# The first tiles behind three inner norms computed from x times its column scale, and another order in the mixer and the drain

## What is computed

```python
def rms_norm_2(x, g):  # x * rsqrt(mean(x*x) + eps) * g
def modulate(h, shift, scale): return h * (1.0 + scale) + shift
mod = silu(c) @ ada_w + ada_b        # shift, scale, gate of three parts, D numbers each
h = modulate(rms_norm_2(x, norm_g[0]), shift0, scale0)
x = x + 0.5 * gate0 * ((silu(h @ Wg) * (h @ Wu)) @ ffn1_w_out)
h = modulate(rms_norm_2(x, norm_g[1]), shift1, scale1)
x = x + gate1 * token_mixer(h)
h = modulate(rms_norm_2(x, norm_g[2]), shift2, scale2)
x = x + 0.5 * gate2 * ffn2(h)
return rms_norm_2(x, final_g)
```

## Time and profile before

| | us |
|---|---|
| median of 3 runs (lowest, highest) | 1940.26 (1938.29, 1940.6) |
| the profiled execution, its own time | 1941.78 |
| its span from first to last instruction | 1939.9 |
| busy: TensorE / VectorE / ScalarE / GpSimd | 1882.2 / 932.9 / 800.3 / 125.6 |
| mean granted clock of TensorE | 0.987 |

### The profile page before, as it was taken

How to read it: one execution, slowest core, us unless ns; L and a number is a source line. 1 busy time by engine, 2 the same in 40 slices (tenths; PEclk the granted TensorE clock), 3 DMA queues, 4 the chain that set the end, 5 groups by cost and what they waited for, 6 DMA issues and landing times.

```text
span 1939.9 us, 22192 instructions
## 1 busy us (share of the span) xinstructions
PE 1882.2 (97%) x8907; PEld 1457.4 (75%) x8907; DVE 932.9 (48%) x1665; ACT 800.3 (41%) x1301; POOL 125.6 (6%) x148
## 2 busy tenths in 40 slices
PE   7999999999999899999998999999999999999997
PEld 4666666666788788888886777687788878888886
DVE  4567666665542433333225566854434443333322
ACT  5466656656542332222223655434432332222221
POOL 0111111110001000000000011000000100000000
PEclk8999999999999999999998999999999999999999
DMA  5334333432233132222223222221023322222221
GB/s 207 148 142 152 141 141 142 152 141 89 76 132 108 65 109 98 98 98 90 101 72 125 93 71 92 75 84 44 32 94 114 121 76 97 98 98 95 100 90 63
DMA packets 56525, 201.94 MB, mean 104 GB/s; under 512 B 6478, under 2 KB 6934, under 8 KB 55784
## 3 DMA queue, kind: packets, MB, share of 16 engines
q1 hardware_dynamic: 44616, 158.32, 23.3%
q0 software_dynamic: 11808, 42.21, 5.9%
HBM read 195.23 MB, written 5.28 MB: 103 GB/s over the span
## 4 chain that ended last, share of the span: by engine, by line
PE 77%; DVE 11%; ACT 9%; issue 2%; DMA 1%; DVEq 0%; SPq 0%; ACTq 0%
PE ps L1016 22%; PE ps L1019 22%; PE ps L1017 22%; ACT wH L1665 2%; DVE wL L1300 2%; PE ps L1105 2%; DVE a L1388 1%; PE ps L1069 1%; DVE a L1544 1%; ACT a L1750 1%; PE ps L1093 1%; PE ps L1081 1%; PE ps L1141 1%; PE ps L1040 1%; DVE g1a L1300 1%
## 5 line engine op out<-in xcount | busy, mean ns | idle before, releaser
L1016 PE MATMUL ps<-hH,wH 128*128 128x512 f32 (+1 forms) x1640 | 667.5, 407 | 19.7 <-DVE hL L1340 12.3
L1019 PE MATMUL ps<-hH,wL 128*128 128x512 f32 (+1 forms) x1640 | 645.6, 394 | 0.7 <-DVE wL L1300 0.7
L1017 PE MATMUL ps<-hL,wH 128*128 128x512 f32 (+1 forms) x1640 | 645.1, 393 | 0.0
L1300 DVE TENSOR_TENSOR wL<-wr,wH 128x1024 fp32r<-128x1024 f32 (+2 forms) x285 | 345.3, 1212 | 579.1 <-ACT wH L1665 579.0
L1665 ACT ACTIVATE wH<-wr 128x1024 fp32r<-128x1024 f32 (+2 forms) x285 | 295.0, 1036 | 265.5 <-PE ps L1019 245.6
L1016 PEld LDWEIGHTS ps<-hH,wH 128*128 128x128 f32 (+1 forms) x1640 | 311.0, 190 | 118.2 <-issue 47.8
L1019 PEld LDWEIGHTS ps<-hH,wL 128*128 128x128 f32 (+1 forms) x1640 | 310.5, 189 | 70.1 <-DVE wL L1300 2.1
L1017 PEld LDWEIGHTS ps<-hL,wH 128*128 128x128 f32 (+1 forms) x1640 | 311.4, 190 | 63.3 <-issue 3.4
L1016 PE MATMUL ps<-gffn,wH 128*128 128x512 f32 x352 | 136.9, 389 | 0.0
L1017 PE MATMUL ps<-gffn,wH 128*128 128x512 f32 x352 | 136.9, 389 | 0.0
L1019 PE MATMUL ps<-gffn,wL 128*128 128x512 f32 x352 | 136.9, 389 | 0.0
(11 more groups left out here) (283 smaller groups left out, 1971.1 us busy)
## 6 DMA issues: line engine op xcount, KB each, us to landing
wr<-wst SPq DMA_DIRECT2D x268, 512.0 KB, 3.4
a<-wfd POOLq DMA_DIRECT2D x54, 512.0 KB, 4.8
xT<-wfd POOLq DMA_DIRECT2D x18, 512.0 KB, 6.6
wr<-wst SPq DMA_DIRECT2D x16, 384.0 KB, 2.9
xT<-xin SPq DMA_DIRECT2D x8, 256.0 KB, 4.8
xT<-xin SPq DMA_DIRECT2D x2, 1024.0 KB, 6.2
xsave<-xT SPq DMA_DIRECT2D x1, 2048.0 KB, 8.9
c<-wfd POOLq DMA_DIRECT2D x8, 256.0 KB, 3.0
```

The lines of the kernel that those rows point to most:

```text
L1016: e.matmul(o, hi, xh[k], start=k == 0, stop=False)
L1017: e.matmul(o, hi, xl[k], start=False, stop=False)
L1019: i = e.matmul(o, lo, xh[k], start=False, stop=k == t.nk - 1)
L1300: e.tensor_tensor(dst, x, hi.bitcast(F32), ALU.subtract).then_inc(s[name], 1)
```

## The change

For the three inner norms the first tiles no longer wait for rs. While the residual tiles run, `raw` makes X[c]*scale (rounded part on ScalarE, rest on VectorE), and `raw_start` issues the first two tiles (three in the feed-forwards) on these; the sum of squares of c=7 stands behind their second k step. The row scale rs is multiplied in at the bank's output, and the shift's part comes as a bias: `shift_row` (eight chained operations 128x128 on VectorE, from the raw weights) and `shift_sum` (fp32 matmuls with ones) give shift*W for each such tile. The usual norm is made beside these tiles, in two halves (`norm_c`) with a weight split between. At n=2 the raw parts lie in hH and hL themselves, so `norm_c` on ScalarE waits for the products of each k (`rm`).

In the same change: `sq_lo` and `rstd` of the last two heads' outputs 4 steps later; pool tiles 0 and 1 of the mixer raw, `feed_pool` behind them, and the save of x behind `baturn`; `l2_sum` 3 ticks later, `l2` 2, `l2_end` 3, `prep_x` 3, `prep_k` and `prep_q` 2, `sol_send` 2, `solve` spread over 90 in place of 75 ticks, `sol_back` and `inverse` 18 later; three banks (6, 7, 0) for `rec_o`; the sum of the squares of n=1 in a tile of its own; one semaphore for several in two places.

```diff
+    def raw(self, n, c):
+        self.add("raw", n=n, c=c, rh=self.sig("rh"), rl=self.sig("rl"))
+    def shift_row(self, n, i, slot):
+        self.add("shift_row", n=n, i=i, slot=slot, wb=self.sig("wb"))
+    def shift_sum(self, n, count):
+        self.add("shift_sum", n=n, count=count, rows=self.count["wb"], modt=self.sig("modt"), wb=self.sig("wb"))
+        self.shb = self.count["wb"]
+    def raw_start(self, n, t0, t1, t2=None):
+        tiles = [t for t in (t0, t1, t2) if t is not None]
+        self.slot(t0, 0)
+        self.slot(t1, 0)
+        for k in range(8):
+            if k == 2:
+                self.last_square()
+                self.raw(n, 7)
+            self.add("mm", t=t0, k=k)
+            self.add("mm", t=t1, k=k, raw=self.sig("rm") if k < 7 else None)
+        if t2 is not None:
+            self.slot(t2, 0)
+            for k in range(8):
+                self.add("mm", t=t2, k=k)
+        for t in tiles:
+            t.done = t.slots[-1] + 1
+        rs = self.sig("rs")
+        self.add("norm_rs", n=n, stat=8 + 2 * n, rs=rs)
+        self.add("norm_c", n=n, c0=0, c1=5, rs=rs, raw=t1)
+        self.add("split", j=t0.slots[0] + NSPL)
+        self.add("norm_c", n=n, c0=5, c1=8, rs=rs, raw=t1)
+        self.add("split", j=t1.slots[0] + NSPL)
+        for name in ("nv", "nh", "nl"):
+            self.count[name] = self.count.get(name, 0) + 8
+        for i, t in enumerate(tiles):
+            if i == 2:
+                self.add("split", j=t2.slots[0] + NSPL)
+            self.add("out_" + t.kind, t=t, done=t.done, raw=i, rs=rs, last=tiles[-1].done, shb=self.shb, **t.more)
...
-                put(0, sq_lo, o3, "o")
-                put(SCHED["o"], rstd, None, o3)
+                put(0 if o3 < HEADS - 2 else 4, sq_lo, o3, "o")
+                put(SCHED["o"] if o3 < HEADS - 2 else 9, rstd, None, o3)
...
+        first = len(self.slots) + 16
+        more = {4: [lambda: add("mod_rest"), lambda: self.raw(1, 0), lambda: self.raw(1, 1)],
+                5: [lambda c=c: self.raw(1, c) for c in (2, 3, 4)], 6: [lambda: self.raw(1, 5)], 7: [lambda: self.raw(1, 6)]}
+        at = {(6, 9): lambda: self.shift_row(1, 0, first), (7, 1): lambda: self.shift_row(1, 1, first + 1),
+              (7, 8): lambda: self.shift_row(1, 2, first + 2), (7, 13): lambda: self.shift_sum(1, 3)}
         for c in range(8):
             r = sig("xr")
-            self.whole(Tile("res0", src("l0_w_out", 128 * c, 16), self.pb01.take()[1], "g", ("xr", r), c=c, xr=r),
-                       then=(lambda: square(c - 1)) if c > 0 else None)
+            t = Tile("res0", src("l0_w_out", 128 * c, 16), self.pb01.take()[1], "g", ("xr", r), c=c, xr=r)
+            for k in self.steps_of(t):
+                if k == 5 and c > 0:
+                    square(c - 1)
+                    for fn in more.get(c, []):
+                        fn()
+                if (c, k) in at:
+                    at[c, k]()
...
+        self.raw_start(n, gate(0, "r"), up(0, "r"), gate(1, "r"))
+        self.whole(up(1))
+        for j in range(2, 22):
+            self.whole(gate(j))
+            self.whole(up(j))
...
+        first = len(self.slots) + 24
         for c in range(8):
             r = sig("xr")
-            self.whole(Tile("res", src(w_out, 128 * c, 22), pb.take()[1], "a", ("xr", r), c=c, xr=r, sub=sub, f=f, back=None),
-                       then=(lambda: square(c - 1)) if c > 0 else None)
-        square(7)
+            t = Tile("res", src(w_out, 128 * c, 22), pb.take()[1], "a", ("xr", r), c=c, xr=r, sub=sub, f=f, back=None)
+            for k in self.steps_of(t):
+                if k == 5 and c > 0:
+                    square(c - 1)
+                    if n == 1:
+                        self.raw(2, c - 1)
+                if n == 1 and c == 7 and k in (2, 9):
+                    self.shift_row(2, k // 9, first + k // 9)
+                if n == 1 and c == 7 and k == 16:
+                    self.shift_sum(2, 2)
+        self.last_square = lambda: square(7)
...
-        self.two(pool(0), pool(1))
+        self.raw_start(n, pool(0, "r"), pool(1, "r"))
+        add("feed_pool")
         t = Tile("ba", src("mix_w_in_2", 4608, cols=16), wk.take()[1], "h", ("bd", 1), n=n)
         self.whole(t)
         for k in self.steps_of(pool(2)):
             if k == 5:
                 pool_mid(0)
         add("baturn", bank=wk.take()[1])
+        self.move("saved")
...
-                at(end + 10 + j, l2_sum, h, l2s)
+                at(end + 13 + j, l2_sum, h, l2s)
                 if which == "k":
-                    at(end + 16 + 2 * j, prep_x, h)
-                    at(end + 34 + 2 * j, prep_k, h)
+                    at(end + 19 + 2 * j, prep_x, h)
+                    at(end + 36 + 2 * j, prep_k, h)
                 else:
-                    at(end + 36 + 2 * j, prep_q, h)
-            at(end + 15, l2, which, l2s)
-            at(end + 23, l2_end, which, l2s)
+                    at(end + 38 + 2 * j, prep_q, h)
+            at(end + 17, l2, which, l2s)
+            at(end + 26, l2_end, which, l2s)
...
-        at(121, lambda: add("sol_send", pa2=8))
+        at(123, lambda: add("sol_send", pa2=8))
         for k in range(1, 31):
-            at(133 + (5 * k) // 2, lambda k=k: add("solve", k=k))
-        at(209, lambda: add("sol_back"))
+            at(135 + 3 * k, lambda k=k: add("solve", k=k))
+        at(227, lambda: add("sol_back"))
         for g in range(2):
             for j, step in enumerate(("t", "p5", "y5", "p6", "y6")):
-                at(233 + 16 * g + 3 * j, inverse, g, step)
+                at(251 + 16 * g + 3 * j, inverse, g, step)
...
-        rk, ro, rm = Ring([3, 4, 5]), Ring([6, 7]), Ring([1, 2])
+        rk, ro, rm = Ring([3, 4, 5]), Ring([6, 7, 0]), Ring([1, 2])
...
+        def behind(c):
+            square(c)
+            self.raw(3, c)
+            if 3 <= c < 6:
+                self.shift_row(3, c - 3, first + c - 3)
+            elif c == 6:
+                self.shift_sum(3, 3)
         for c in range(8):
             r = sig("xr")
             self.whole(Tile("res", src("mix_w_out_2", 128 * c), pb6.take()[1], "m", ("xr", r), c=c, xr=r, sub=1, f=None,
-                            back=c // 4), then=(lambda: square(c - 1)) if c > 0 else None)
-        square(7)
+                            back=c // 4), then=(lambda: behind(c - 1)) if c > 0 else None)
+        self.last_square = lambda: square(7)
...
+        def raw_views(n):
+            if n == 2:
+                return rhs["h"]
+            a = ff[0]["aH"][0:16] if n == 1 else ff[1]["aH"][16:22] + ff[1]["aL"][0:10]
+            return a[0:8], a[8:16]
+        def shift_rows(n, i):
+            return {1: row1, 2: ff[0]["row"], 3: tq[1]}[n][:, 128 * i:128 * i + 128]
...
+                if t.rhs == "r":
+                    w.wait_ge(s["rl"], 8 * (t.more["n"] - 1) + k + 1)
...
+                elif what == "shift_sum":
+                    b = take(6)
+                    bank_free[6] = ("wb", d["wb"])
+                    w.wait_ge(s["wb"], d["rows"])
+                    for j in range(d["count"]):
+                        i = e.matmul(b[:, 2 * j:2 * j + 2], shift_rows(d["n"], j), C("one", 0, 2), start=True, stop=True)
+                    i.then_inc(s["modt"], 1)
...
+                elif what == "raw":
+                    n, c = d["n"], d["c"]
+                    xh, xl = raw_views(n)
+                    w.wait_ge(s["rh"], d["rh"])
+                    e.scalar_tensor_tensor(xl[c], X[c], scale_col(n, c), xh[c].bitcast(F32),
+                                           ALU.mult, ALU.subtract).then_inc(s["rl"], 1)
+                elif what == "shift_row":
+                    n, j = d["n"], d["slot"]
+                    v, acc = split_views(j)[0], shift_rows(n, d["i"])
+                    w.wait_ge(s_raw[j % NRAW], 16 * (j // NRAW + 1))
+                    own(e.tensor_scalar(acc, v[:, 0:128], shift_col(n, 0), None, ALU.mult, ALU.bypass))
+                    for k in range(1, 8):
+                        own_done()
+                        i = e.scalar_tensor_tensor(acc, v[:, 128 * k:128 * k + 128], shift_col(n, k), acc, ALU.mult, ALU.add)
+                        if k < 7:
+                            own(i)
+                    i.then_inc(s["wb"], 1)
+                elif what == "shift_sum":
+                    w.wait_ge(s["modt"], d["modt"])
+                    e.tensor_copy(shb[:, 0:2 * d["count"]], ps[6][:, 0:2 * d["count"]]).then_inc(s["wb"], 1)
+                elif what == "norm_c":
+                    n, c0, c1 = d["n"], d["c0"], d["c1"]
+                    rs, tmp = norm_views(n)
+                    w.wait_ge(s["rs"], d["rs"])
+                    for c in range(c0, c1 + 1):
+                        if c < c1:
+                            if c >= 2:
+                                w.wait_ge(s["nl"], 8 * n + c - 1)
```

(53 more changed lines are left out.)

117 lines of the change are left out of this document (68 added, 49 removed).

## The result

The median after is 1914.70 us (1914.08 to 1916.92, 4 runs) beside 1940.01 us (4 runs) of the kernel before: a ratio of 0.9873, 95% interval 0.9856 to 0.9890, so 25.3 us less. The forecast was 1910.6, 29.7 less. The profiled execution after took 1915.1 us (span 1913.3), 26.7 less than the one before. The sum came out near, in part by luck: one of its six terms, the mixer's events with 8.8 us, was worth nothing, and four of the others paid more than I had put down.

A forecast was written before the change was run, and what follows sets the result against it. TensorE was taken as the bound, so only its idle or slow time could be won. The terms 3.2 + 3.3 + 6.7 + 8.8 + 4.3 + 3.4 = 29.7 us gave median 1910.6 us, range 1905 to 1918 (8 in 10: 1903 to 1922).

The forecast's parts named there:

- the mixer's events: Mixer: l2_sum 3 ticks later removes most of four waits for squares and slow products: 8.8 us, ends 4.5 and 10.
- What bounds it: Whole kernel: TensorE, busy 1882 of 1939.9 us, is the bound; only its idle or slow time can be won.
- n=1: Norm behind out0: raw start gains 8.1 us, less shift sum, a wait and slow clock: net 3.2, ends 1.9 and 7.3.
- n=2: Norm before the mixer: two raw tiles, waits for pool weights and baturn's copy: net 3.3 us, ends 1.1 and 6.1.
- n=3: Norm behind the mixer: raw start gains 8.1 us, less 0.8 and 0.6: net 6.7, ends 4 and 7.3.
- The drain and the bank: Drain: later sq_lo and rstd, 4.3 us (2.5 to 4.6); recurrence: third bank removes three waits, 3.4 us (at least 2).
- My own line on what would prove me wrong: Wrong if a split waits within 12 us of a norm, clock falls without a pause, or l2 waits move elsewhere.
- A: At n=1 and n=2 the clock stays up and pool weights come in time: 35 us gain, 1905; chance 0.17.
- B: VectorE takes the norm's place: boundaries lose 1.5 us and a clock fall each, l2's fourth wait stays: 1925; chance 0.10.
- C: Only mixer and drain count; raw starts wait for their own rows, boundaries give 0: 16.5 us gain, 1924; chance 0.07.
- D: Whole kernel slower: without pauses the chip lowers TensorE's clock; 250 slow products give 1961 us; chance 0.02.

The follow-up runs named there:

- the other ring: Changed kernel plus taps ahead of the weight split, solve and inverse earlier, n=1 column sum at k=15, n=3 PSUM ring from bank 2: 1903.30 us, ratio 0.9812.
- prep early: Changed kernel with prep_k and prep_q two ticks earlier, at end + 34 and end + 36: 1915.46 us, ratio to before 0.988.
- sum at k=15: Changed kernel with the shift's column sum at n=1 at k=15 instead of k=13 of the last tile: 1911.75 us, ratio to before 0.9863.

## Why the prediction came out as it did

*What bounds it*: right for the whole. TensorE was and is the bound, and the gain is what it no longer idles or runs slowly. Not right for the sessions of the mixer, where ScalarE and VectorE together set the pace (42.95 against 41.5 us).

*n=1*: 3.2 forecast, 3.8 measured. The wait before the shift sum, its reason and the clock's fall behind it were as worked out; the wait was 1.7 us instead of 2.1, since VectorE met no add of GpSimd there, and eight products were slow instead of ten. In the one execution without the fall the stage gave 5.0.

*n=2*: 3.3 forecast, 5.7 in this trace and 4.2 where the clock fell behind the wait for the weights. The three waits of the 16-column tile were two, 1.7 instead of 2.3. The pool weights were there at T+27.6, where I had 28.2. The copy for baturn ended at T+29.4, where I had 29.6 (my terms add to 29.5), but TensorE came to it only at T+30.0 and waited for nothing. I had put one stretch of low clock behind the wait for the weights; in after it lay ahead, from 1034.28 on, and the wait swallowed it.

*n=3*: 6.7 forecast, 6.0 measured. No wait at the shift sum. The 0.6 that I took off for VectorE's lateness did turn up as 0.98, at a place that I hadn't looked at: the residual that frees the second tile's bank. The experiment with the other ring shows it (1.27 us by starts).

*The drain and the bank*: 4.3 and 3.4 forecast, 4.5 and 4.2 measured, the same alone by stage. The bank's term was the sum in the table of waits, which leaves out some 0.3 us of each pause.

*The mixer's events*: 8.8 forecast, below even my lower end of 4.5; 1.2 against the profile before, and -0.2 against three kernels with the old ticks. This is the step that failed: "Moving l2_sum by 3 ticks of three products is 2.05 us of TensorE's time. Three of the four waits are 1.0 to 1.3 us and go whole." I took four waits for four separate latenesses, each to be covered by the same 2.05 us. They were one: the chain of ScalarE and VectorE fell behind TensorE by about 1.4 us a session. A later l2_sum is covered once; what it doesn't wait in session 1 is missing in session 2. The waits of after show it (none, 0.4, 1.2, 1.8), and what the shift did save went to two new waits, at v_turn and at the inverse, with slow products behind the latter. The numbers for this stood in the trace of before: the ends of the waits for the squares are 42.93 us apart, and the copies on ScalarE follow the squares without an idle for TensorE. My own line on what would prove me wrong, "the l2 waits at another line, such as prep_k", named the sign, not the reason.

*The rivals*: A (the clock stays up) doesn't hold for after, where it fell at n=1, n=2 and the inverse; at n=1 it held in one of the six kernels with that wait. B named VectorE, but behind the norms, where no split was late; with ScalarE in turn it was the bound in the mixer. C is refuted by the raw starts alone, 13.4 us. D didn't show: the mean clock rose from 0.987 to 0.994.

*The Trainium skill* (SBUF — State Buffer, Terms) has the pair of ports that VectorE and GpSimd share locked for a whole instruction; at its worst, a meeting with all of GpSimd's add, that would have made the wait at n=1 2.9 us. No meeting fell on that row: its seven operations took 2.67 us, 0.38 each. Elsewhere the trace agrees with a lock, and shows its price. L1455 takes 0.75 us alone and 1.51 to 1.79 in its thirteen meetings with an add of GpSimd in after; 0.96 to 1.24 us of the add were left at its start, and each time it ended 0.55 us behind the add. So a meeting cost what was left of the add less 0.2 us. At 1538.47, for one, L1455 took 1.52 us with 0.97 left of the add that began at 1537.90. The operation of 1.42 us from which I took 0.67 fits this too: 0.87 us of the add were left, and it ended 0.55 behind.

## What to carry to other kernels

When one engine waits several times in a row for the same producer, first put the ends of those waits side by side. If they are evenly spaced and the spacing is longer than the consumer's own work in between, it is a rate, and a later place of the consumer pays once at most; look for work that sits in the producer's turn only because of its queue's order. And when a change has several parts, run each alone: of six parts with 26.7 us together one was worth nothing, and the total, near its forecast, didn't show it.

## What the runs showed beside

The length of a pause did not decide whether the clock fell. Behind the same wait in kernels that are alike there, it fell in some executions (products at 0.43 instead of 0.23 us from start to start) and stayed at 1.00 in others:

| wait | clock fell behind it | clock stayed up |
|---|---|---|
| 1.69 us, n=1 | five kernels | one (prep early) |
| 1.12 and 0.58 us, 16-column tile of n=2 | four | five |
| 1.50 us, inverse | four | one (sum at k=15) |

It also stayed at 1.00 behind 1.78 us before the last l2_sum of after and behind 1.5 before the pool weights; it fell in all five that waited 2.8 or 2.9 us there, the ones where it had stayed up at the 16-column tile. What tells these apart is open. A forecast of one execution is uncertain by such falls, up to 1.6 us each here.
